# A two-stack transformer kernel: attention's small products spread, its maxima put ahead of scalings, unread products added, and the last gated unit on fewer tokens

## The reference, cut to what matters

```python
def forgetting_attention(q, k, v, log_f):       # a part of the mixer, 8 heads of 64
    F = jnp.cumsum(log_f, axis=1).transpose(0, 2, 1)
    def attend(start, end):
        s = jnp.einsum("bqhd,bkhd->bhqk", q[:, start:end], k[:, :end]) * scale
        s = s + F[:, :, start:end, None] - F[:, :, None, :end]
        s = jnp.where(mask, s, NEG_INF)
        return jnp.einsum("bhqk,bkhd->bqhd", jax.nn.softmax(s, axis=-1), v[:, :end])
    outs = [attend(0, N_META)]                  # the 16 meta tokens, a block of their own
    ...                                         # then four blocks of 128 tokens

def ffn_sublayer(h, pre_g, post_g, w_up, conv_w, w_down):
    u = rms_norm(h, pre_g)
    z = jnp.einsum("bld,df->blf", u, w_up)                  # 1024 -> 5632
    z = causal_depthwise_conv(z, conv_w)                    # 3 taps over the tokens
    g, up = jnp.split(z, 2, axis=-1)
    y = jnp.einsum("blf,fd->bld", jax.nn.silu(g) * up, w_down)   # 2816 -> 1024
    return h + rms_norm(y, post_g)
...
    return h[:, N_META:]                        # the end of the first stack
```

## Time and profile before

| | |
|---|---|
| median of three runs | 2962.5 us (2960.69 to 2965.73) |
| the profiled execution, its own time | 2958.24 us |
| its span, from the first to the last instruction | 2956.4 us |
| TensorE busy | 2853.4 us, 97% |
| VectorE, ScalarE, GpSimd busy | 1404.8, 1070.8, 220.9 us |
| mean granted clock of TensorE | 0.978 |
| attention of the first layer, first score to the next stage | 188.3 to 279 us |
| attention of the second layer | 917.0 to 1006 us |
| gated unit of the second layer: ups, downs, layer's end | 1080 to 1338, to 1466, to 1482 us |

### The profile page before, as it was taken

One profiled execution on the slowest core, in us unless ns is written; L12 is line 12 of the kernel. 1 busy time (PEld: TensorE's weight loads), 2 busy tenths in 40 slices (PEclk: granted clock), 3 DMA queues, 4 the chain that ended last, 5 costly groups with the idle time before them and its releaser, 6 DMA issues. The chain is left out here.

```text
span 2956.4 us, 46483 instructions
## 1 busy us (share of the span) xinstructions
PE 2853.4 (97%) x18586; PEld 2449.9 (83%) x18586; DVE 1404.8 (48%) x2277; ACT 1070.8 (36%) x1496; POOL 220.9 (7%) x206
## 2 busy tenths in 40 slices
PE   8999999999999999999999999999999999999998
PEld 7986899999897789999988656788878755688886
DVE  3743477741574257773242554433424365343342
ACT  3244433322324444332233344432423334342332
POOL 0001300001000120000100022000010002200000
PEclk9989999999998999999999899999999989999999
DMA  3200322222120032222242101222223200122222
GB/s 125 100 29 16 131 91 85 85 97 88 63 100 15 30 136 85 85 82 97 77 140 93 58 1 43 86 100 100 99 86 105 106 31 2 58 86 100 99 89 110
DMA packets 44784, 237.04 MB, mean 80 GB/s; under 512 B 4894, under 2 KB 14750, under 8 KB 21872
## 3 DMA queue, kind: packets, MB, share of 16 engines
q1 hardware_dynamic: 34976, 222.09, 21.5%
q10 hardware_dynamic: 9680, 13.17, 1.3%
HBM read 233.09 MB, written 11.59 MB: 83 GB/s over the span
## 5 line engine op out<-in xcount | busy, mean ns | idle before, releaser
L161 PE MATMUL psum<-u_up_a_hi,w_a_hi 128*128 128x264 f32 x1408 | 376.2, 287 | 5.3 <-DVE u_up_a_lo L1895 5.0
L162 PE MATMUL psum<-u_up_a_lo,w_a_hi 128*128 128x264 f32 x1408 | 373.3, 285 | 0.0
L152 DVE TENSOR_TENSOR w_mlp_b_lo<-ring,w_mlp_b_hi 128x1024 fp32r<-128x1024 f32 x128 | 157.0, 1226 | 330.4 <-ACT w_mlp_b_hi L145 330.4
L164 PE MATMUL psum<-u_up_a_hi,w_a_lo 128*128 128x264 f32 x1408 | 286.1, 284 | 0.0
L152 DVE TENSOR_TENSOR w_a_lo<-ring,w_a_hi 128x1024 fp32r<-128x1024 f32 (+1 forms) x154 | 187.1, 1216 | 206.8 <-ACT w_a_hi L145 204.2
L161 PEld LDWEIGHTS psum<-u_up_a_hi,w_a_hi 128*128 128x128 f32 x1408 | 265.1, 188 | 13.1 <-DVE u_up_a_lo L1895 9.7
L145 ACT ACTIVATE w_a_hi<-ring 128x1024 fp32r<-128x1024 f32 (+1 forms) x154 | 161.4, 1049 | 295.8 <-PE psum L164 294.6
L162 PEld LDWEIGHTS psum<-u_up_a_lo,w_a_hi 128*128 128x128 f32 x1408 | 264.7, 188 | 0.1
L145 ACT ACTIVATE w_mlp_b_hi<-ring 128x1024 fp32r<-128x1024 f32 x128 | 135.7, 1060 | 300.3 <-PE psum L164 299.6
L164 PEld LDWEIGHTS psum<-u_up_a_hi,w_a_lo 128*128 128x128 f32 x1408 | 219.5, 189 | 0.0
L161 PE MATMUL psum<-u_up_b_hi,w_mlp_b_hi 128*128 128x512 f32 x512 | 199.6, 390 | 1.0 <-DVE u_up_b_lo L502 1.0
(11 more groups left out here) (457 smaller groups left out, 6450.4 us busy)
## 6 DMA issues: line engine op xcount, KB each, us to landing
ring<-in_wup SPq DMA_DIRECT2D x44, 1024.0 KB, 4.9
ring<-in_wup_b SPq DMA_DIRECT2D x32, 1024.0 KB, 4.8
ring<-in_wdown_b SPq DMA_DIRECT2D x32, 1024.0 KB, 4.8
ring<-in_win SPq DMA_DIRECT2D x22, 1024.0 KB, 4.9
ring<-in_wdown SPq DMA_DIRECT2D x32, 704.0 KB, 4.1
ring<-in_win_b SPq DMA_DIRECT2D x12, 1024.0 KB, 4.8
near_copies<-near_rows ACTq DMA_DIRECT2D x2, 4608.0 KB
ring<-in_wout SPq DMA_DIRECT2D x8, 1024.0 KB, 5.0
```

The lines of the kernel that those rows point to most:

```text
L152: nc.vector.tensor_tensor(W["lo"][:, buf, 0:n], W["tiles"][:, slot, at:at + n], W["hi"][:, buf, 0:n].bitcast(F32), ALU.subtract).then_inc( ...
L161: nc.tensor.matmul(out[c], a_hi, b_hi, start=start, stop=False)
L162: nc.tensor.matmul(out[c], a_hi, b_lo, start=False, stop=False)
L164: mm = nc.tensor.matmul(out[c], a_lo, b_hi, start=False, stop=stop)
```

## The change

In both layers' attention:

- The third part of `meta` becomes `meta_values(pair)`: two products each, issued ahead of the products of `score(1, 1)` to `score(1, 4)`, behind these scores' waits. They go into columns 400 to 463 of banks 0 and 1. VectorE's copy of them (`copy_meta`) moves behind `split_maxima(1)`. `transposed(0, 1)` waits for the fifth step of `meta_dve` in place of the sixth; `turn_top(1)`, which writes all of bank 0, now waits for the sixth.
- `keep_clock(n)` issues n products of 512 columns into banks 6 and 7 that nobody reads: 5 ahead of `meta(0)`, 4 ahead of `score(1, 0)` (behind a new wait for the fourth `head_log`, which reads these banks), 3 behind `transposed(0, 0)`.
- VectorE's `head_scale(0)` moves behind `maxima(2, 0)`, `head_scale(1)` to `(3)` move behind `maxima(2, 1)` to `(2, 3)`. `head_scale(4)` moves behind `maxima(3, 0)`.

In the second layer's gated unit and layer end only (`tokens_used`): the input side takes tokens 12 to 527 (516, two pieces of 258), and everything from the taps on takes 16 to 527 (512, one piece).

```diff
+def tokens_used(layer):
+    return (META - 4, META) if layer == DEPTH - 1 else (0, 0)
...
                 pass_waits(pe, S)
+                if pair == 1 and u:
+                    meta_values(u - 1)
                 out = [ps[:, score_bank(pair, u, h), 0:b - a] for h in range(2)]
...
-                    pe.wait_ge(meta_dve.sem, meta_dve.at(layer, 6))
+                    pe.wait_ge(meta_dve.sem, meta_dve.at(layer, 5))
...
+            def keep_clock(n):
+                for b in range(n):
+                    nc.tensor.matmul(ps[:, 6 + b % 2, :], ident_r, fixed[:, 4 * P:8 * P], start=True, stop=True)
...
+            keep_clock(5)
             meta(0)
...
             meta(1)
+            pe.wait_ge(hn_ln.sem, hn_ln.at(layer, 4))
+            keep_clock(4)
             score(1, 0)
             for pair in range(PAIRS):
                 for jj in range(K):
                     transposed(pair, jj)
-                    if (pair, jj) == (0, 0):
-                        meta(2)
...
+                    if (pair, jj) == (0, 0):
+                        keep_clock(3)
...
+                    else:
+                        pe.wait_ge(meta_dve.sem, meta_dve.at(layer, 6))
                     turn_top(pair + 1)
...
                     for u in range(1, K):
                         maxima(pair + 1, u)
+                        if pair == 1 and u < 4:
+                            head_scale(u)
                     split_maxima(pair + 1)
+                    if pair == 0:
+                        copy_meta()
                     rows_of_maxima(pair + 1)
...
-                if pair == 0:
-                    for i in range(4):
-                        head_scale(i)
-                else:
-                    head_scale(3 + pair)
                 if pair + 1 < PAIRS:
                     copy_mixed(pair)
                 if pair + 2 < PAIRS:
                     maxima(pair + 2, 0)
+                head_scale(3 + pair if pair else 0)
...
-                                 [(u_hi[:, k, c0:c0 + cn], u_lo[:, k, c0:c0 + cn]) for c0, cn in chunks(TA)],
+                                 [(u_hi[:, k, t0 + c0:t0 + c0 + cn], u_lo[:, k, t0 + c0:t0 + c0 + cn]) for c0, cn in chunks(n_in)],
...
-                                 [(hid[0][:, kx + k, c0:c0 + cn], hid[1][:, kx + k, c0:c0 + cn]) for c0, cn in chunks(TA)],
+                                 [(hid[0][:, kx + k, c0:c0 + cn], hid[1][:, kx + k, c0:c0 + cn]) for c0, cn in chunks(n_out)],
```

More of the change, by code:

```diff
@@ L538, in _, with add_scaled @@
                                                op0=ALU.mult, op1=ALU.mult).then_inc(made, 1)
-def add_scaled(nc, dve, S, layer, use, k, y, gain):
-    nc.vector.scalar_tensor_tensor(out=y[:, k, :], in0=y[:, k, :], scalar=gain[:, k:k + 1], in1=S["rstd"][:, :],
-                                   op0=ALU.mult, op1=ALU.mult).then_inc(S["res_scaled"].sem, 1)
-def add_to_h(nc, pool, S, layer, use, k, y, h):
+def add_scaled(nc, dve, S, layer, use, k, y, gain, first):
+    nc.vector.scalar_tensor_tensor(out=y[:, k, first:TA], in0=y[:, k, first:TA], scalar=gain[:, k:k + 1],
+                                   in1=S["rstd"][:, first:TA], op0=ALU.mult, op1=ALU.mult).then_inc(S["res_scaled"].sem, 1)
@@ L561, in mean_of, with root_of @@
                               start=(k == 0), stop=(k == KD - 1))
     return mm
-def root_of(nc, act, S, layer, use):
+def root_of(nc, act, S, layer, use, first):
+    n, rstd = TA - first, S["rstd"][:, first:TA]
     act.wait_ge(S["res_summed"].sem, S["res_summed"].at(layer, use + 1))
-    nc.scalar.activation(split(S["rstd"][:, :], TA), banks(S["psum"], 6, TA), ACT.Ln,
+    nc.scalar.activation(split(rstd, n), banks(S["psum"], 6, n), ACT.Ln,
                          bias=S["eps6"][:, 0:1]).then_inc(S["res_rooted"].sem, 1)
@@ L588, in _ @@
                 if k < KD:
-                    add_scaled(nc, dve, S, layer, 1, k, y, gain)
+                    add_scaled(nc, dve, S, layer, 1, k, y, gain, first)
                 if k >= 1:
                     dve.wait_ge(scaled.sem, scaled.at(layer, KD + k))
-                    nc.vector.tensor_tensor(h[:, k - 1, :], h[:, k - 1, :], y[:, k - 1, :], ALU.add).then_inc(added.sem, 1)
+                    nc.vector.tensor_tensor(h[:, k - 1, first:TA], h[:, k - 1, first:TA], y[:, k - 1, first:TA],
+                                            ALU.add).then_inc(added.sem, 1)
         @block.scalar
@@ L599, in _ @@
                 act.wait_ge(added.sem, added.at(layer, KD + k + 1))
-                nc.scalar.activation(y[:, k, :], h[:, k, :], ACT.Square).then_inc(S["res_sq"].sem, 1)
-            root_of(nc, act, S, layer, 1)
+                nc.scalar.activation(y[:, k, first:TA], h[:, k, first:TA], ACT.Square).then_inc(S["res_sq"].sem, 1)
+            root_of(nc, act, S, layer, 1, first)
         @block.tensor
@@ L606, in _ @@
             for k in range(KD):
-                mm = mean_of(nc, pe, S, layer, 1, k, y)
+                mm = mean_of(nc, pe, S, layer, 1, k, y, first)
             mm.then_inc(S["res_summed"].sem, 1)
@@ L646, in fox_stage @@
     PAIRS, K = HEADS_A // 2, FOX_STEPS
-    SLOTS = 3
+    SLOTS, META_OUT = 3, 400
     hn_sq, hn_pe, hn_ln, hn_root, hn_dve, hn_high = (
@@ L1005, in _, with copy_meta @@
             nc.vector.tensor_copy(meta_pt[:, :], ps[0:META, 5, 0:P]).then_inc(meta_dve.sem, 1)
-            dve.wait_ge(meta_pe.sem, meta_pe.at(layer, 3))
-            for h in range(2):
-                rows = slice(DH * h, DH * (h + 1))
-                at = P + META * PAIRS * h
-                last = nc.vector.tensor_copy(y[rows, 0:PAIRS, 0:META],
-                                             ps[rows, 5, at:at + PAIRS * META].rearrange("p (n c) -> p n c", c=META))
-            last.then_inc(meta_dve.sem, 1)
+            def copy_meta():
+                dve.wait_ge(meta_pe.sem, meta_pe.at(layer, 3))
+                for h in range(2):
+                    rows = slice(DH * h, DH * (h + 1))
+                    last = nc.vector.tensor_copy(y[rows, 0:PAIRS, 0:META],
+                                                 ps[rows, h, META_OUT:META_OUT + PAIRS * META].rearrange("p (n c) -> p n c", c=META))
+                last.then_inc(meta_dve.sem, 1)
             maxima(1, 0)
@@ L1686, in glu_stage_a @@
     sq, total = S["y_square"], S["y_total"]
+    t0, o0 = tokens_used(layer)
+    n_in, n_out = TA - t0, TA - o0
+    sq, total = sq[:, 0:n_out], total[:, 0:n_out]
     with nc.Block() as block:
@@ L1707, in lot @@
                     cols = slice(k * UNIT, (k + 1) * UNIT)
-                    mm = product(nc, [ps[:, 2 * j + c, 0:cn] for c, (_, cn) in enumerate(chunks(TA))],
+                    mm = product(nc, [ps[:, 2 * j + c, 0:cn] for c, (_, cn) in enumerate(chunks(n_in))],
                                  (W["hi"][:, j % 2, cols], W["lo"][:, j % 2, cols]),
-                                 [(u_hi[:, k, c0:c0 + cn], u_lo[:, k, c0:c0 + cn]) for c0, cn in chunks(TA)],
+                                 [(u_hi[:, k, t0 + c0:t0 + c0 + cn], u_lo[:, k, t0 + c0:t0 + c0 + cn]) for c0, cn in chunks(n_in)],
                                  k == 0, k == KD - 1)
                     if fresh:
-                        mean = mean_of(nc, pe, S, layer, 0, k, y)
+                        mean = mean_of(nc, pe, S, layer, 0, k, y, t0)
                 if fresh:
```

75 lines of the change are left out of this document (40 added, 35 removed).

## The result

The changed kernel took 2940.38 us, the median of four runs (2930.09 to 2941.41), against 2961.6 us of the kernel before beside it (2956.72 to 2965.73): a ratio of 0.9917, interval 0.9900 to 0.9934. The prediction was 2926.9 us, with a range of 2916 to 2947: faster, as forecast, and inside the range, but 13.5 us slower than its number. The median fell by 21.2 us where 35.6 were forecast. The same kernel, run twice more in the experiments, gave 2943.27 us (eight runs, ratio 0.9935) and 2946.23 us (ten runs, 0.9954).

The account below looks back on a forecast made before the run. TensorE was taken to bound the kernel, by columns streamed and clock: 4.2 - 0.7 + 12.7 + 7.8 + 14.3 = 38.3 us, less one clock fall, 35.6. From the 2962.5 us median this gave 2926.9 us, range 2916 to 2947.

Parts of the forecast that it names:

- The head: Attention's start to the turn of pair 0's maxima: 11.4 us at full clock, gain 4.2 us over both layers.
- Ahead of pair 0: Four unread products in a 0.72 us gap: 0.2 to 0.9 us lost per layer, 0.35 taken, 0.7 in all.
- Pair 0: First attention pair, from its transposed to the next pair's: 17.6 us at full clock, gain 12.7 us for both layers.
- Pair 1: Second attention pair becomes like the third, 16.57 us with a 0.30 us wait: gain 7.8 us for both layers.
- The unit: Second layer's gated unit on fewer tokens: 14.3 us gained, with 8.4 in `down` and 5.2 in the ups.
- Entry and end: The gated unit's entry and the layer's end, with fewer columns per tile: 0.7 us gained.
- The sum without a fall: All terms together if the clock holds through every stretch: 38.3 us gained.
- I don't count on six of six and take one fall of 2.7 us: Six joints between attention pairs, three per layer: one clock fall costing 2.7 us, leaving 35.6 us gained.
- the clock falls all the same: Rival: unread products too few in pair 0 or ahead of it; 2946.4 us, chance 0.12.
- VectorE late: Rival: GpSimd holds up the scalings moved between the maxima, up to 7.6 us; 2934.5 us, chance 0.10.
- ups gain nothing: Rival: the pace of the gated unit's up-projection isn't set by columns; 2932 us, chance 0.07.
- slower by pieces at columns 12 and 270: Rival: TensorE reads the ups' pieces slower from these starts, 63 us for 2112 products; 2995 us, chance 0.03.

Follow-up runs that it names:

- e4: The changed kernel without its 12 unread products and without the wait for the fourth head log: 2953.47 us.
- e7: The kernel before with only VectorE's head scalings moved behind the maxima: 2954.78 us, ratio 0.9987.
- e5: The changed kernel with the second layer's gated result in rows of 512 columns, not 528: 2929.08 us, one run.
- e12: The changed kernel run a third time, no edit: 2946.23 us, ten runs, ratio 0.9954.
- e1: The changed kernel run again, no edit: 2943.27 us, eight runs, ratio 0.9935.
- e2: The attention part of the change alone, the last gated unit as in the kernel before: 2948.78 us.
- e10: The changed kernel with 512-column rows for the gated result and 544-column rows for the ups' operand, first used token at column 16 in layer two: 2935.10 us, one run.
- e9: The changed kernel with 512-column rows for the second layer's gated result and 20 more unread products where the clock fell: 2932.44 us, ratio 0.9896.
- e8: The changed kernel with the meta value products back in one lump and VectorE's copy of them ahead of the maxima: 2942.54 us.

## Why the prediction came out as it did

- **The head.** 11.3 and 11.4 us for the forecast's 11.4, at full clock: right, and in e4's profile, without the five products, the head's clock is 0.76 again.
- **Ahead of pair 0.** From the turn to the first transposed 2.71 us for 2.17 before: a loss of 0.54 a layer, for 0.35 taken, inside the bounds. A batch of unread products costs some 0.2 us more than its products.
- **Pair 0.** 18.7 us for 17.6. The third pair, taken as the pattern, has no `score(p+2, 0)`, which pairs 0 and 1 do; pair 1 shows that this costs 0.33. The batch is 0.21 more, and the meta values 0.5 to 0.55 a group for 0.45. That is 0.7 to 0.9 of the 1.1 us; the rest is open. Gain 10.5 for 12.7 us.
- **Pair 1.** 16.9 for 16.57, the same missing score: 7.2 for 7.8. The mechanism was right, and e7 shows it without the rest of the change.
- **The unit.** `down` 5.8 for 8.4: the term used the second stack's 225.4 ns for a product whose rows are longer, and in e5 2.4 of the missing 2.6 us come back. The ups 3.6 for 5.2: products without stalls fell from 122.3 to 120.2 ns, 2.0 and not 2.5 each, 4.2 us over 2078 of them, and the wait at the end of each round of the loop grew from some 0.31 to 0.42 us and took 0.7 back. Entry and end gave about what was said.
- **The sum without a fall** was 38.3; the profiled executions give 28.2 (2958.24 to 2930.09). 3.0 are missing in attention, 4.2 in the unit's two terms, and 4.0 went in the second stack, at a lower clock there. These are 11.2 for the 10.1 that are missing; 1.1 was gained between the windows.
- **The number and the range.** The medians gained 21.2 us for 35.6. The 14.4 us between them are the 10.1 above; 7.6 more, since the median lies 10.3 above the profiled execution and one fall of 2.7 had been taken; less 3.4, by which the profiled execution before lay under its median. The range held since the rivals' times had been put into it, and only just: e12's median, 2946.23 us, is 0.8 us inside its end.
- **The step that failed** is "I don't count on six of six and take one fall of 2.7 us". Of the twelve attention layers profiled with the changed list (the result, e1, e2, e5, e10, e12), the clock fell in pair 0 in four and at pair 2 in one. A fall in pair 0 isn't worth one joint's 2.7 us but 9.8 to 13.9 us (from the turn of pair 0 to that of pair 3), since the following pairs begin low or fall again. 15 of the 22 executions are 10 us or more above the best one, and the three medians 10 to 16 us; how much of that fell in attention only the profiled ones show. The rival "the clock falls all the same" had the mechanism and the place, and at 0.12 far too small a chance; it is not all or nothing, as it was written, but a matter of the single execution. What decides it from one execution to the next stays open. That its 2946.4 us is nearly e12's median is luck: it had the head without gain, which gained in full.
- **What the change is worth**, from the equal-clock column: 9.7 us of work, nearly all of it the unit's (8.4), and a median clock of 0.980 for 0.977, 6.6 us; together 16.3 us of span over 78 and 22 executions. Attention's part works nearly by the clock alone: the waits that it saves are filled with unread products.
- **VectorE late, ups gain nothing, slower by pieces at columns 12 and 270**: none happened. Products of 258 columns on such starts are cheaper than those of 264 (120.2 against 122.3 ns).

## What to carry to other kernels

Where TensorE's clock decides, one profile is one draw: read the mean clock of every execution, and compare kernels at an equal clock before a few us are put down to an edit. Waits aren't the only weak places: see in several profiles where the clock falls (here behind small products without a wait of note), and put unread products there, ahead of and behind it, not only where the longest wait was (e9, five executions). A time per product holds only for the same row length of its operand: 231.2 and 226.7 ns here.

## What the hardware showed unexpectedly

- TensorE fell to the lower clock in a stretch that was 94% busy (e12) and stayed low for much of one without idle time (e8's pair 0, 26.60 of 26.60 us busy at a mean of 0.62). Small products and half the rows are what these stretches have in common; that they are the cause is not shown.
- The same list of instructions kept or lost the clock from one layer to the other of one execution (18.67 and 26.07 us).
- A product of 512 columns costs 226 or 227 ns with rows of 512 columns, and 225 to 236, each place its own, with rows of 528.
- Batches of three, four or five unread products took 0.21, 0.22 and 0.14 us beyond their streaming time.
